# A three-stage fp32 kernel: the last layer's norm moved into factors, its transposes moved into the projection before it, and the pooling products reordered

## The chip, the core and the metric

The kernel runs on one core of one Trainium2 chip. The metric is the device time of one execution in microseconds (us), from the first instruction to the last on that core, with a small part around it. The engines are named as the profile names them: PE is the matrix engine (TensorE), PEld its weight loads, DVE the vector engine, ACT the scalar (activation) engine, POOL GpSimd, and SP the engine that issues nearly all transfers. Everything is fp32. In the trace one fp32 matmul of the program is two rows (two passes over the moving operand); a transpose is one row.

## The reference

The input `x` is 256 tokens by 1024 features. It passes through one block (a gated delta-rule mixer, a mixture of 32 experts, a gated embedding) and then two more layers. Only the ends of the chain matter here, where the change is:

```python
# first mixer: per-token gates are 64 of the input projection's columns
qkv, z, ab = jnp.split(x @ w_in, [GDN_CONV_CH, GDN_CONV_CH + GDN_VAL_WIDTH], axis=-1)
...
def even_layer(x, g_norm, w_in, conv_w, b_if, g_head, w_pool, s_pool, w_out):
    ...
    h = rmsnorm(h, g_head).reshape(bsz, s_len, A_WIDTH).astype(x.dtype)
    y_a = h * jax.nn.silu(z_a)
    pooled = multiscale_pool(u).astype(x.dtype)
    y_b = jnp.einsum('bsgc,gcd->bsgd', pooled, w_pool).reshape(bsz, s_len, B_WIDTH)
    y_b = y_b * s_pool * jax.nn.silu(z_b)
    return x + jnp.concatenate([y_a, y_b], axis=-1) @ w_out

def odd_layer(x, g_norm, w_in, g_kv, w_uk, w_uv, g_q, g_k, w_out, rel_bias):
    xn = rmsnorm(x, g_norm)
    p = xn @ w_in
    q, ckv, qi, ki, wi, z = _split(p, ODD_SPLITS)
    q = rmsnorm(q.reshape(hd), g_q)
    ckv = rmsnorm(ckv, g_kv)
    ...
    return x + (out * jax.nn.silu(z)) @ w_out
```

In the part of the odd layer that is left out, index scores pick 64 keys for each token, and attention runs over those. `rmsnorm` divides each token's row by the root of its mean square. `pooled` has four groups of 256 channels, each with a window of its own; `w_pool` is a 256x256 matrix for each group.

## The kernel before, in words

The program is written out by hand: each engine has its own list of instructions, and `wait_ge` on a semaphore is the only thing that orders them against each other. Nothing is scheduled by a planner; on each engine the order in the source is the order on the chip. Tokens lie in two tiles of 128 (`NT` is 2), features in eight tiles of 128 (`KT` is 8). The accumulators are eight banks of 512 columns, `bank(b)`. Weights come in units of 1 MB (1024x256) into slots; `fill` in `odd_sync`, `even_sync` and elsewhere has SP wait until a slot's last unit is multiplied and then issue the transfer of the next one. SP's list is in order too.

**The start** (`gdn_tensor`, L596 to L606). PE first computes the per-token gates (64 columns): 16 matmuls with tokens as the stationary operand and 64 moving columns (L601). Then come the four halves of head 0's query and key projection (`project_half`, L449, 16 matmuls with 256 moving columns). Then the sums over the gates (L613 on), for which DVE and ACT have meanwhile made the decays.

**The even layer's end** (`even_tensor` from L2264, `even_scalar` from L2356, `even_vector` from L2461). For each of the four groups, PE multiplies by the window matrix (pooling, L2271), ACT copies the bank to SBUF (L2359), and PE multiplies by the group's mixing matrix (L2279); DVE multiplies the result by the silu gate (L2465). After the last group ACT squares the heads (L2368) and makes the root of the mean (L2371, L2373), and DVE scales and gates the heads (L2471). The pooled half `zb` and the head half `za` are transposed by PE (`turn_tensor`, L267) and copied by ACT with a per-feature scale (`turn_scalar`, L281) into `yt`. Only then does the output projection start (`project`, L251): four groups of 256 columns, each with 32 matmuls over both halves of `yt`. DVE adds each group to the residual `x` (L2477).

**The odd layer's head** (`odd_sync` from L2536, `odd_tensor` from L2555, `odd_scalar` from L2755, `odd_vector` from L2874). When the last group is added, SP issues four small transfers and ACT squares all of `x` (L2181) and makes the root. DVE scales `x` by it (L2876), PE transposes the result (L267), ACT copies it with the per-feature weight (L281), and PE multiplies: a small bias product (L2560), the index queries (L2567), the index keys (L2571) and index weights (L2575, 4 moving columns each), and the compressed keys (L2580). The index scores (L2591) follow, then the query projection (L2603), the attention loop with the gate projection in between (L2634), and the output projection (L2695). `keep_gates` (L2808, L2809) brings one unit of the gate projection from its bank to SBUF, once as it is and once through Exp.

## Time and profile before

| What | Value |
|---|---|
| Runs | 1180.51, 1181.7 and 1182.4 us; median 1181.7 us |
| The profiled execution | 1179.04 us, of which 1177.4 us are the span in the trace |
| PE | busy 1076.1 us, 91% of the span |
| DVE, ACT, POOL | busy 33%, 30% and 4% of the span |
| Chain that ended last | PE 76%, SP's queue 10%, DVE 5%, ACT 4%, DMA 3% |
| Mean granted clock of PE | 0.962 of full speed |

The profiled execution took 2.7 us less than the median of the three runs. The chain is read back from the last instruction: at each step to what released it, or to the instruction before it on its engine. It runs through PE nearly everywhere; the question for an edit is where it leaves PE.

### The profile page before, as it was taken

What the parts mean: (1) busy time and instruction counts of PE and PEld (TensorE: products, weight loads), DVE (VectorE), ACT (ScalarE), POOL (GpSimd) and SP (SyncE); (2) the same over time, 40 slices, a digit from 0 to 9 for tenths busy, and PEclk for the clock granted to TensorE, in tenths of its full rate; (3) what the DMA queues carried; (4) which work ended last, traced back from release to release, by engine and by line L of the source; (5) the groups of instructions that cost most, each with busy time, mean ns of one, the idle gap of its engine ahead of it and who ended that gap; (6) DMA issues with size and microseconds to landing.
All of it is one profiled execution on the core that took longest, in us unless ns stands there. A gap on an engine that the chain in (4) does not pass through costs nothing.

```text
span 1177.4 us, 24312 instructions
## 1 busy us (share of the span) xinstructions
PE 1076.1 (91%) x10643; PEld 821.0 (70%) x10643; DVE 391.3 (33%) x937; ACT 354.0 (30%) x988; POOL 43.8 (4%) x47
## 2 busy tenths in 40 slices
PE   7999999999899999887777999999999797999989
PEld 6776777767677884433332788888887686776877
DVE  2555565555552143100000444420001100083760
ACT  2654554644644221110001131031112501033440
POOL 0110000000000000000000000000000000032000
PEclk9999999999999999988888999999999898799989
DMA  6233233233217477999999633434443144431211
GB/s 261 71 138 118 74 119 118 74 118 109 110 45 303 147 275 301 421 421 424 423 422 424 272 105 131 143 112 168 149 144 107 71 149 174 109 143 72 108 36 36
DMA packets 40030, 210.40 MB, mean 179 GB/s; under 512 B 5344, under 2 KB 14432, under 8 KB 15984
## 3 DMA queue, kind: packets, MB, share of 16 engines
q1 hardware_dynamic: 39920, 208.80, 46.7%
q8 instruction: 86, 1.41, 0.5%
q14 instruction: 24, 0.20, 0.1%
HBM read 207.67 MB, written 1.11 MB: 177 GB/s over the span
## 4 chain that ended last, share of the span: by engine, by line
PE 76%; SPq 10%; DVE 5%; ACT 4%; DMA 3%; issue 2%; ACTq 0%; DVEq 0%
SPq L236 10%; PE ps L2299 9%; PE ps L449 9%; PE ps L251 7%; PE ps L452 4%; PE ps L2205 4%; PE ps L2695 3%; PE ps L769 2%; PE ps L2603 2%; PE ps L780 2%; PE ps L2036 2%; DMA arena<-in_wu 2%; PE ps L2634 2%; PE ps L505 2%; PE ps L1541 2%
## 5 line engine op out<-in xcount | busy, mean ns | idle before, releaser
L449 PE MATMUL ps<-xt,slots 128*128 128x256 f32 x512 | 127.1, 395 | 0.0
L2299 PE MATMUL ps<-slots,yt 128*128 128x256 f32 x512 | 110.7, 379 | 0.0
L449 PEld LDWEIGHTS ps<-xt,slots 128*128 128x128 f32 x512 | 94.7, 194 | 19.6 <-issue 7.5
L2299 PEld LDWEIGHTS ps<-slots,yt 128*128 128x128 f32 x512 | 97.2, 190 | 13.2
L251 PE MATMUL ps<-slots,yt 128*128 128x256 f32 x384 | 83.4, 379 | 1.0 <-ACT yt L281 1.0
L251 PEld LDWEIGHTS ps<-slots,yt 128*128 128x128 f32 x384 | 72.8, 190 | 11.0 <-ACT yt L281 1.2
L1541 PE MATMUL ps<-arena 128*32 128x512 f32 x280 | 56.5, 693 | 23.4 <-DMA arena<-in_wu 9.1
L452 PE MATMUL ps<-slots,xt 128*128 128x256 f32 x256 | 64.5, 395 | 0.0
L1092 DVE SCALAR_TENSOR_TENSOR arena<-arena 128x256 f32<-128x256 f32 x128 | 56.2, 485 | 0.3
L452 PEld LDWEIGHTS ps<-slots,xt 128*128 128x128 f32 x256 | 46.5, 192 | 10.6 <-issue 4.3
L1541 PEld LDWEIGHTS ps<-arena 128*32 128x32 f32 x280 | 15.3, 124 | 53.0 <-issue 53.0
L1541 PE MATMUL ps<-slots,arena 128*32 128x512 f32 x160 | 46.2, 734 | 4.4 <-DMA xt<-in_wu 4.4
L2205 PE MATMUL ps<-yt,slots 128*128 128x256 f32 x224 | 49.0, 380 | 0.0
L2205 PEld LDWEIGHTS ps<-yt,slots 128*128 128x128 f32 x224 | 42.3, 190 | 6.1 <-issue 0.4
L3000 POOL TENSOR_TENSOR arena<-arena 128x512 f32<-128x512 f32 (+1 forms) x8 | 17.8, 2260 | 711.2 <-DVE arena L2895 711.2
L2347 ACT ACTIVATE arena<-ps,rms 128x256 f32<-128x256 f32 x32 | 13.4, 471 | 90.2 <-PE ps L2299 90.2
L2459 DVE SCALAR_TENSOR_TENSOR arena<-ps,arena 128x256 f32<-128x256 f32 x8 | 3.2, 477 | 108.5 <-ACT arena L2355 108.5
L1641 ACT ACTIVATE arena<-ps 128x256 f32<-128x256 f32 x8 | 3.1, 386 | 115.1 <-PE ps L1541 115.1
L1314 POOL TENSOR_TENSOR arena<-arena 128x256 f32<-128x256 f32 x32 | 24.3, 761 | 311.7 <-ACT arena L835 193.2
L1862 DVE TENSOR_TENSOR arena<-arena,ps 128x256 f32<-128x256 f32 x8 | 3.4, 422 | 94.0 <-ACT arena L1641 94.0
L2634 PE MATMUL ps<-slots,xt 128*128 128x256 f32 x128 | 31.9, 395 | 1.2 <-ACT arena L2802 1.2
L769 PE MATMUL ps<-slots,yt 128*128 128x256 f32 x128 | 31.0, 389 | 0.0
(397 smaller groups left out, 1788.0 us busy)
## 6 DMA issues: line engine op xcount, KB each, us to landing
slots<-in_wu SPq DMA_DIRECT2D x114, 1024.0 KB, 4.8
arena<-in_wu SPq DMA_DIRECT2D x58, 1024.0 KB, 26.1
yt<-in_wu SPq DMA_DIRECT2D x10, 1024.0 KB, 26.4
xt<-in_wu SPq DMA_DIRECT2D x4, 1024.0 KB, 26.5
arena<-bias_rows SPq DMA_DIRECT2D x1, 2048.0 KB, 14.7
arena<-delta_rows SPq DMA_DIRECT2D x14, 128.0 KB, 7.6
xt<-in_xt SPq DMA_DIRECT2D x2, 512.0 KB, 4.9
x<-in_x SPq DMA_DIRECT2D x1, 1024.0 KB, 8.1
```

The lines of the kernel that those rows point to most:

```text
L236: SP.dma_start(self.slot(slot), self.ins["wu"][unit]).then_inc(*self.arrived[slot].up())
L251: q = M.matmul(self.bank(base + cg, UC, t * UC), lhs[:, h * KT + k, t * P:(t + 1) * P], self.slot(s)[:, k, :], start=(t == 0 and k == 0 an ...
L449: q = M.matmul(bank(n, T), self.slots[:, s, k, n * P:(n + 1) * P], self.xt[:, k, :], start=(k == 0), stop=(k == KT - 1))
L452: q = M.matmul(bank(n, UC), folded(k, n), self.slots[:, s, k, :], start=(k == 0), stop=(k == KT - 1))
L769: q = M.matmul(self.out_bank(t, cg), self.yt[:, k, t * P:(t + 1) * P], self.slots[:, s, k, :], start=((cg % 2 == 0 or (t, cg) == (1, 3)) a ...
L1092: q = V.scalar_tensor_tensor(g.cn[:, s], src, w, g.cn[:, s], ALU.mult, ALU.add)
L1314: G.tensor_tensor(by_cc(g.mt), by_cc(g.ac), g.lvt[:, l].unsqueeze(1).to_broadcast([P, 2, 128]), ALU.mult).then_inc(*g.masked.up())
L1541: q = M.matmul(self.ps[r, 2, :], g.xg[:, half * (KT // 2) + k, r], self.flat(slots[e])[:, k * 512:(k + 1) * 512], start=(half == 0 and k = ...
L2205: q = M.matmul(bank(s, T, T * n), self.slots[:, s, k, n * P:(n + 1) * P], self.xe[:, k, :], start=(k == 0), stop=(k == KT - 1), skip_group ...
L2299: q = M.matmul(self.bank(s, UC, t * UC), self.xe[:, k, t * P:(t + 1) * P], self.slots[:, s, k, :], start=(t == 0 and k == 0), stop=(k == K ...
L2634: q = M.matmul(bank(g.z_banks[u], UC, t * UC), self.xt[:, k, t * P:(t + 1) * P], self.slots[:, u, k, :], start=(t == 0 and k == 0), stop=( ...
L2695: q = M.matmul(bank(g.out_banks[i], UC, t * UC), self.xt[:, k, t * P:(t + 1) * P], self.slots[:, i, k, :], start=(t == 0 and k == 0), stop ...
```

## The change

1. **Start.** The gates are computed with the 64 gate columns as the stationary operand and all 256 tokens moving (8 matmuls), copied by DVE (L1216 of the new file) and transposed back by PE (L607) after a quarter of the first projection.
2. **Pooling ahead of mixing.** The pooling product of the next group stands ahead of the mixing product of each group, in `even_tensor`.
3. **Heads' root later, table earlier.** ACT's activation table with Ln and Exp is loaded once after the sigmoid. ACT copies the transposed `zb` before it makes the heads' root.
4. **Output projection begins with the pooled half.** It is split into half units (8 matmuls each, `out_half`), with an own bank for each column group. Three of them stand ahead of the transposes of `za`. The weights are fetched in the order in which the slots come free now.
5. **Raw x turned.** `turn_columns` transposes each group of `x` as soon as its residual is added, between half units; ACT copies with the norm's per-feature weight, and squares the group.
6. **The norm as factors.** The odd layer's products use `x` without the division by the root. Each consumer gets the factor: index keys by a product with a row of factors (spread by 2 matmuls, L2647 of the new file), index weights by the factor squared, the gates by a per-token scale in `keep_gates`, and the query and compressed-key norms by an epsilon scaled with the token's mean square.
7. The index weights and the small bias table are loaded during the even layer; the mask constants and feature weights stay where the even layer has them.

The diff, cut to its core:

```diff
@@ -596,14 +597,18 @@
         for half in range(2):
             M.wait_ge(*g.xt_in[half](1))
-            for cc in range(2):
-                for k in range(4 * half, 4 * half + 4):
-                    q = M.matmul(bank(2, 64, cc * 64), folded(k, cc), g.wab[:, k, :],
-                                 start=(cc == 0 and k == 0), stop=(k == KT - 1), skip_group_check=True)
+            for k in range(4 * half, 4 * half + 4):
+                q = M.matmul(ps[0:64, 3, 0:T], g.wab[:, k, :], self.xt[:, k, :], start=(k == 0), stop=(k == KT - 1))
+        q.then_inc(*g.gates_f.up())
+        project_half(0, 0, 0)
+        M.wait_ge(*g.gates_fk(1))
+        M.wait_ge(*g.common(3))
+        for cc in range(2):
+            q = M.transpose(bank(2, 64, cc * 64), g.sq[0:64, 0, tile(cc)], ident[0:64, 0:64])
         q.then_inc(*g.gates.up())
-        for j in range(2):
-            for part in range(2):
-                project_half(0, j, part)
+        project_half(0, 0, 1)
+        project_half(0, 1, 0)
+        project_half(0, 1, 1)
...
@@ -2168,22 +2181,14 @@
+        SP.wait_ge(*g.scores(1))
+        SP.dma_start(self.wki[:, :, :], I["w_ki"]).then_inc(*self.odd_in.up())
+        SP.dma_start(self.rb[:, :], I["rel_bias_2"]).then_inc(*self.odd_in.up())
         for s in (4, 5):
             self.fill(s, U_CKV + s - 4)
-        for i in range(2):
-            for s in range(4):
+        for i, order in enumerate(((1, 3, 0, 2), (1, 0, 3, 2))):
+            for s in order:
                 self.fill(s, U_EOUT + 4 + 4 * i + s)
...
@@ -2279,14 +2290,62 @@
+        pool(0)
+        pool(1)
+        mix(0)
+        pool(2)
+        mix(1)
+        pool(3)
+        mix(2)
+        mix(3)
...
+        def out_half(cg, h, t):
+
+            s = (2 * cg + h) % 4
+            if t == 0:
+                M.wait_ge(*self.arrived[s](self.multiplied[s].n + 1))
+            for k in range(KT):
+                q = M.matmul(bank(cg, UC, t * UC), self.yt[:, h * KT + k, t * P:(t + 1) * P], self.slots[:, s, k, :],
+                             start=(h == 1 and t == 0 and k == 0), stop=(h == 0 and k == KT - 1), skip_group_check=True)
...
         M.wait_ge(*g.zb_made(4))
         M.wait_ge(*g.hn_made(2))
-        self.turn_tensor(g.pj[:, 2], KT, [6, 7], g.zb_turned, g.zb_kept)
+        self.turn_tensor(g.pj[:, 2], KT, [4, 5, 6, 7], g.zb_turned, g.zb_kept)
+        M.wait_ge(*g.zb_kept(4))
+        out_half(0, 1, 0)
+        out_half(0, 1, 1)
+        out_half(1, 1, 0)
         M.wait_ge(*g.za_made(1))
-        self.turn_tensor(g.pj[:, 1], KT, [4, 5], g.za_turned, g.za_kept)
+        self.turn_tensor(g.pj[:, 1], KT, [4, 5, 6, 7], g.za_turned, g.za_kept)
+        out_half(1, 1, 1)
         M.wait_ge(*g.za_kept(4))
-        g.out_done = self.project(self.yt, 8, 2, self.even_added)
+        for cg in range(2):
+            out_half(cg, 0, 0)
+            out_half(cg, 0, 1)
+        self.turn_columns(0)
+        for cg in range(2, 4):
+            out_half(cg, 1, 0)
+            out_half(cg, 1, 1)
+            self.turn_columns(cg - 1)
+            out_half(cg, 0, 0)
+            out_half(cg, 0, 1)
+
+    def turn_columns(self, c):
+
+        M = self.nc.tensor
+        M.wait_ge(*self.even_added(c + 1))
+        for j in range(2):
+            for t in range(NT):
+                q = M.transpose(self.bank(4 + c, P, j * T + t * P), self.x[:, t, (2 * c + j) * P:(2 * c + j + 1) * P],
+                                self.c["ident"])
+        q.then_inc(*self.x_turned.up())
...
@@ -2353,6 +2412,7 @@
         A.activation(g.pj[:, 3], g.pj[:, 3], ACT.Sigmoid).then_inc(*g.o_sig.up())
+        A.preload_act_table_set("natural_log_exp_and_others")
...
@@ -2535,11 +2605,6 @@
-        SP.wait_ge(*self.even_added(4))
-        SP.dma_start(g.late_at, I["c_late"]).then_inc(*g.loaded.up())
-        SP.dma_start(g.wki[:, :, :], I["w_ki"]).then_inc(*g.loaded.up())
-        SP.dma_start(g.feat[:, :], I["feat"]).then_inc(*g.loaded.up())
-        SP.dma_start(g.rb[:, :], I["rel_bias_2"]).then_inc(*g.loaded.up())
...
@@ -2554,19 +2619,21 @@
-        M.wait_ge(*g.xn_made(1))
-        self.turn_tensor(g.xn, KT, [0, 1], g.turned, g.xt_kept)
-        M.wait_ge(*g.loaded(4))
...
+        for cg in range(4):
+            M.wait_ge(*self.x_kept(cg + 1))
+            for n in range(2):
+                for k in (2 * cg, 2 * cg + 1):
+                    q = M.matmul(bank(5, T, n * T), self.slots[:, 5, k, n * P:(n + 1) * P], self.xt[:, k, :],
+                                 start=(n == 0 and k == 0), stop=(k == KT - 1), skip_group_check=True)
+            if cg == 0:
+                self.turn_columns(3)
...
+        M.wait_ge(*g.diag_made(1))
+        for t in range(NT):
+            q = M.matmul(bank(0, P, t * P), c["ones"], g.diag[:, t], start=True, stop=True, skip_group_check=True)
+        q.then_inc(*g.r_spread.up())
...
@@ -2805,8 +2880,11 @@
-            A.activation(g.pq[:, 1, :, cols], self.two(g.z_banks[u]), ACT.Copy)
-            A.activation(g.pq[:, 0, :, cols], self.two(g.z_banks[u]), ACT.Exp, scale=-1.0).then_inc(*g.z_kept.up())
+            for t in range(NT):
+                src = bank(g.z_banks[u], UC, t * UC)
+                A.activation(g.pq[:, 1, t, cols], src, ACT.Copy, scale=r[:, t:t + 1])
+                q = A.activation(g.pq[:, 0, t, cols], src, ACT.Exp, scale=g.neg[:, t:t + 1])
+            q.then_inc(*g.z_kept.up())
...
@@ -2871,11 +2951,23 @@
         V.wait_ge(*g.st_exp(1))
         for t in range(NT):
-            q = V.tensor_scalar(g.xn[:, t], self.x[:, t], g.st[:, t:t + 1], None, ALU.mult)
-        q.then_inc(*g.xn_made.up())
-        V.wait_ge(*g.loaded(4))
+            q = V.tensor_scalar(g.diag[:, t], c["ident"], r[:, t:t + 1], None, ALU.mult)
+        q.then_inc(*g.diag_made.up())
+        V.tensor_scalar(g.neg[:, :], r, -1.0, None, ALU.mult)
+        V.scalar_tensor_tensor(g.rr[:, :], r, IH ** -0.5, r, ALU.mult, ALU.mult).then_inc(*g.rr_made.up())
+        V.wait_ge(*g.index_kept(1))
+        V.wait_ge(*g.r_spread(1))
+        V.tensor_tensor(g.kit[:, :], g.kit[:, :], bank(0, T), ALU.mult).then_inc(*g.kit_made.up())
```

How the edits move instructions is seen in three pieces of the engines' lists. PE at the even layer's end, before: L2271 pools, L2279 mixes, L267 transposes both halves of `yt`, L251 is the output projection.

```order
L2279 MATMUL ps<-slots,arena 128x256 x4
L2271 MATMUL ps<-slots,arena 128x256 x4
L2279 MATMUL ps<-slots,arena 128x256 x4
L267 MATMUL ps<-cst,arena 128x128 x32
L251 MATMUL ps<-slots,yt 128x256 x128
```

The same place in the changed kernel: L2290 mixes, L267 transposes `zb` and then `za`, L2311 is `out_half`, L2346 transposes raw `x`, and L2630 is the index query product of the odd layer.

```order
L2290 MATMUL ps<-slots,arena 128x256 x8
L267 MATMUL ps<-cst,arena 128x128 x16
L2311 MATMUL ps<-slots,yt 128x256 x24
L267 MATMUL ps<-cst,arena 128x128 x16
L2311 MATMUL ps<-slots,yt 128x256 x40
L2346 MATMUL ps<-cst,x 128x128 x4
L2311 MATMUL ps<-slots,yt 128x256 x16
L2346 MATMUL ps<-cst,x 128x128 x4
L2311 MATMUL ps<-slots,yt 128x256 x32
L2346 MATMUL ps<-cst,x 128x128 x4
L2311 MATMUL ps<-slots,yt 128x256 x16
L2630 MATMUL ps<-xt,slots 128x256 x4
```

The 128 matmuls of the projection are still 128, but 24 of them stand ahead of the second 16 transposes, and 12 of the 16 transposes for the odd layer stand among them.

PE at the odd layer's head, before (L267 transposes the normed `x`):

```order
L267 MATMUL ps<-cst,arena 128x128 x16
L2560 MATMUL ps<-arena 16x512
L2567 MATMUL ps<-xt,slots 128x256 x16
L2571 MATMUL ps<-xt,arena 128x256 x8
L2575 MATMUL ps<-arena,xt 128x4 x16
L2580 MATMUL ps<-slots,xt 128x256 x16
```

And in the changed kernel, from the index query product on:

```order
L2630 MATMUL ps<-xt,slots 128x256 x4
L2346 MATMUL ps<-cst,x 128x128 x4
L2630 MATMUL ps<-xt,slots 128x256 x12
L2635 MATMUL ps<-arena 16x512
L2638 MATMUL ps<-xt,arena 128x256 x8
L2642 MATMUL ps<-arena,xt 128x4 x16
L2647 MATMUL ps<-arena,cst 128x128 x2
L2651 MATMUL ps<-slots,xt 128x256 x16
```

Four transposes are left here, after the first quarter of the index queries; the small bias product stands behind them, and two matmuls that spread the factors are new.

ACT from the pooled copies on, before (L281 copies transposed blocks, L2181 squares `x`):

```order
L2359 ACTIVATE arena<-ps 128x512 x4
L2368 ACTIVATE arena<-arena 128x256 x8
L2371 ACT_TABLE_LOAD
L2371 ACTIVATE arena<-arena,cst 128x8
L2373 ACT_TABLE_LOAD
L2373 ACTIVATE arena<-arena 128x8
L281 ACTIVATE yt<-ps,arena 128x256 x16
L2757 ACT_TABLE_LOAD
L2181 ACTIVATE arena<-x 128x1024 x2
L2184 ACTIVATE arena<-arena,cst 128x2
L2186 ACTIVATE arena<-arena 128x2
L281 ACTIVATE xt<-ps,arena 128x256 x8
```

And in the changed kernel (L2439 copies a column group of transposed `x`, L2443 squares it; both come four times, of which one is shown):

```order
L2415 ACT_TABLE_LOAD
L2419 ACTIVATE arena<-ps 128x512 x4
L2428 ACTIVATE arena<-arena 128x256 x8
L281 ACTIVATE yt<-ps,arena 128x256 x8
L2432 ACTIVATE arena<-arena,cst 128x8
L2434 ACTIVATE arena<-arena 128x8
L281 ACTIVATE yt<-ps,arena 128x256 x8
L2439 ACTIVATE xt<-ps,arena 128x256 x2
L2443 ACTIVATE arena,rms<-x 128x256 x2
```

One table load ahead of the copies takes the place of three behind the squares, and the copies of `zb` stand ahead of the root.

## Rows read from the trace of the kernel before

**Rows 1.** The page's first line.

```profile
span 1177.4 us, 24312 instructions
```

**Rows 2.** Timeline, first 22 us: start, duration, engine, line, operation, count.

```profile
5.06 0.43 SPq L373 DMA_DIRECT2D arena<-in_gdn_norm_w  x1
...
5.79 7.06 PE L601 MATMUL ps<-arena,xt 128*128 128x64 f32 x32 [5.79 <-DMA xt<-in_xt]
...
12.64 8.34 PE L449 MATMUL ps<-xt,slots 128*128 128x256 f32 x32
...
15.02 0.19 DVE L1228 COPY arena<-arena 64x64 f32<-64x64 f32 x1
...
20.91 0.28 PE L613 MATMUL ps<-arena 64*64 64x16 f32 x2
```

**Rows 3.** Weight loads at the start, by line: min/median/max ns, first and last start.

```profile
L601 PEld LDWEIGHTS ps<-arena,xt x32: 285/333/333, 5.8 to 12.3; 128*128 128x128 f32 x32
L449 PEld LDWEIGHTS ps<-xt,slots x32: 190/190/337, 12.5 to 20.4; 128*128 128x128 f32 x32
```

**Rows 4.** Transfers, first 40 us and 895 to 1035 us: KB, median us to landing.

```profile
arena<-in_gdn_norm_w SPq DMA_DIRECT2D x1, 0.5 KB, 6.8
...
slots<-in_wu SPq DMA_DIRECT2D x13, 1024.0 KB, 4.8
```

**Rows 5.** Chain that ended last, even layer's end: start, duration, what.

```profile
904.26 1.74 PE ps L2271 x8
...
906.68 1.99 PE ps L2279 x8
...
919.75 1.70 ACT arena L2368 x8
...
923.27 1.28 ACT L2371
...
926.42 3.27 DVE arena L2471 x8
...
934.56 55.53 PE ps L251 x256
```

**Rows 6.** Timeline of the same stretch: DVE gates, PE transposes, ACT copies.

```profile
921.93 0.69 DVE L2465 TENSOR_TENSOR arena<-arena,ps 128x512 f32<-128x512 f32 x1 [3.72 <-PE ps L2279]
...
922.67 1.09 PE L267 MATMUL ps<-cst,arena 128*128 128x128 f32 x8 [0.78 <-DVE arena L2465]
...
926.30 1.55 ACT L281 ACTIVATE yt<-ps,arena 128x256 f32<-128x256 f32 x4
```

**Rows 7.** Chain that ended last, odd layer's head.

```profile
992.32 5.52 DMA arena<-in_rel_bias
...
1000.73 1.81 PE ps L2560 x2
1002.54 10.00 PE ps L2567 x32
1012.54 3.45 PE ps L2571 x16
1016.00 4.12 PE ps L2575 x32
1020.12 9.70 PE ps L2580 x32
```

**Rows 8.** Stretches: us, PE, PEld, DVE, ACT, POOL busy, granted clock, DMA share, GB/s.

```profile
994.70:1008.40 13.70, 11.61 (x32) 8.00 (x33) 0.33 (x1) 3.84 (x9) 0.00 (x0) 0.50 0.34 110
1018.60:1025.40 6.80, 6.80 (x21) 5.72 (x21) 0.00 (x0) 0.94 (x3) 0.00 (x0) 0.50 0.01 3
926.40:933.30 6.90, 5.46 (x23) 4.51 (x24) 3.25 (x8) 5.18 (x13) 0.00 (x0) 0.51 0.00 0
```

**Rows 9.** Chain that ended last, last gate unit in the attention loop.

```profile
1131.88 0.60 ACT arena L2808
...
1132.99 0.44 DVE arena L2931
```

114 lines of the change are left out of this document (72 added, 42 removed).

## The prediction

> **What bounds the kernel now.** I read the page's chain first. It stays on PE for 76% of the span of 1177.4 us [rows 1], so an edit pays only where the chain leaves PE. Then I followed the chain in order of time through the three places that the diff touches.
>
> At the even layer's end it alternates. A pooling product (1.74 us) is followed by ACT's copy of the bank, and the mixing product starts 0.68 us after the pooling product ends; four such rounds take the time from 904.26 to about 919.2 [rows 5]. Then the chain goes over ACT (squares from 919.75, two table loads of 1.28 us between 923.27 and 926.4), over DVE (3.27 us) and over the transposes of the head half, until the output projection starts at 934.56 [rows 5]. It is 55.53 us of PE without a gap, to 990.09. At the odd layer's head PE is off the chain again: the last of four small transfers is issued at 992.32 and lands 5.52 us later, and the first index query matmul stands at 1002.54 [rows 7]. In this stretch PE's granted clock falls: 0.50 from 994.7 to 1008.4, 0.50 again from 1018.6 to 1025.4, and 0.51 from 926.4 to 933.3 [rows 8]. So 1.2 GHz instead of 2.4, and a matmul pass takes twice its time.
>
> Prices of PE's work. At full clock a pass with 256 moving columns is 55.53/256 = 0.217 us [rows 5]. A program matmul is two passes, 0.434 us; eight of them (an `out_half`) are 3.47 us. At half clock a pass is twice that, 0.434. A transpose is 1.09/8 = 0.136 us [rows 6], so four are 0.54 and sixteen 2.2 us.
>
> **The start.** Before, 32 passes with 64 moving columns take 7.06 us, and the four projection halves 8.34 us instead of 32 x 0.217 = 6.9 [rows 2]. Weight loads take 333 ns in the first passes and 190 ns later [rows 3], so PE begins at the pace of half clock, and 8.34 - 6.9 = 1.4 us lost means that the pace doubled 2.8 us after 12.64 less half a pass, near 15. After, 16 passes with 256 moving columns cost 16 x 0.434 = 6.9 us: from 5.79 to 12.7, as long as before. The first half projection is 8 passes, five at the slow pace and the rest at the fast one, to 15.6. The constants that the transposes wait for are in by 5.06 + 6.8 = 11.9 [rows 2, 4], so this wait costs nothing; if the gates were ready at 9.2 it would cost 0 to 1 us. Two transposes, 0.3 us; then 24 passes, 5.2 us: the sums start at 21.1 instead of 20.91 [rows 2]. The gates' own chain on DVE and ACT, which ended at 15.2 for gates made at 12.8, ends near 18.3, ahead of 21.1. Term: **+0.2 us**. When the pace doubles need not stay the same, since PE's work ahead of it is another: if it came at 11.5 instead of 15, 3.5 us of slow work would run in half the time, and the term would be 0.2 - 1.75 = -1.5 us. That is the other bound.
>
> The Trainium skill ("TensorE: Matmul & The Clock Gate", section "What's actually happening") says that the engine's default is the throttled state and that activity releases it. The loads of 333 ns agree [rows 3], although the granted clock is listed as full there.
>
> **The even layer's end.** PE: pool 0, pool 1, mix 0, pool 2, mix 1, pool 3, mix 2, mix 3. Each ACT copy (0.68 us with its hand-over) now lies under another product of 1.74 us, so eight products run on: 8 x 1.74 = 13.9 us, from 904.26 to 918.2. The last gate by DVE (0.69 us, [rows 6]) makes `zb` ready at 918.95. ACT copies the last bank by 915.4 and squares from there for 3.52 us (919.75 to 923.27 before, [rows 5]), to 918.9: just as late as `zb`. The early table load needs 1.28 us beside PE's first pooling and costs nothing; if it were not covered it would cost that. PE transposes `zb`, the first group of four by 919.5, all by 921.2. ACT copies 16 blocks' worth in 8 activations, 2 x 1.55 = 3.1 us [rows 6] plus hand-overs, to 922.9. This is what ends last: the projection starts at **922.9 instead of 934.56, -11.7 us**. Behind the copies, Ln and Exp (0.5 us, no table load between) and DVE's 3.27 us [rows 5] give `za` at 926.7. PE gets there after three half units, 922.9 + 10.4 = 933.3, so 6.6 us are spare.
>
> What moves into the projection: 16 transposes of `za` (2.2 us) and 12 of raw `x` (3 x 0.54 = 1.6). The copies of `za` (3.3 us) lie under half a unit that takes 3.47: cover is just enough, up to 0.3 us could show. ACT's copies and squares of `x` lie under 13.9 us of PE a group. The projection ends at 922.9 + 55.5 + 2.2 + 1.6 = **982.2, against 990.09: -7.9 us**.
>
> The weights: slots 1 and 3 are freed at 929.8 and 938.9, slots 0 and 2 at 945.8 and 952.8, and their next units are wanted at 953.3 and 967.7, 960.7 and 975. A unit lands in 4.8 us [rows 4]; the tightest has 14.9. Nothing is added. SP's new wait on the scores stands behind 28 weight units, long after the scores; the small transfers behind it delay the next unit by an issue each, under the same margin.
>
> **The odd layer's head.** The root, DVE's scaling, twelve transposes, all copies and the four small transfers leave the path. PE goes on: index queries 16 x 0.434 = 6.9, four transposes 0.54 (the last residual add, 0.7 us, is hidden by the first quarter, 1.7), so 989.7; bias product at full clock 1.81/2 = 0.9, to 990.6; index keys 3.45; index weights 4.12 [rows 7]; spreading the factors 0.5, to 998.7. The factors themselves (squares, sums, Ln, Exp on ACT and DVE) end near 988.5. Compressed keys: 9.70 as before [rows 7], if the clock falls again, else 6.9.
>
> I take 9.70; the other bound is 6.9. The fall at 1018.6 came 2.6 us into the 32 passes with 4 moving columns, which ran back to back [rows 7, 8], and those passes are unchanged. So 1008.4 instead of 1029.8: this part gives 39.7 - 26.2 = **-13.5 us**. Of that, 4.0 is clock (the index queries from 10.00 to 6.9, the bias product from 1.8 to 0.9); the rest is idle time and transposes.
>
> The same page of the Trainium skill has the clock fall for an idle PE. The row speaks against it, since PE was not idle before 1018.6. By the page there would be no fall and the term would be 2.8 us larger.
>
> DVE's scaling of the index keys (0.4 us, after ACT's copies by 999.7) is hidden by the compressed keys. From the scores on all waits keep their distances: selection on DVE, bias tiles and weights are all started by events that move along.
>
> **The tail.** Copies of the gates are four activations of 256 columns instead of two of 512: 1.55 [rows 6] instead of about 1.1 (1131.88 to 1132.99, [rows 9]). The last one is on the chain, for DVE and ACT alike. **+0.5 us**; if all four counted, +1.9. The second Ln for the queries and for the compressed keys (0.3 each) lie beside 7 us and more of PE.
>
> **Sum.** +0.2 - 7.9 - 13.5 + 0.5 = -20.7 us. On the profiled execution that is 1179.04 - 20.7 = 1158.3; that one took 2.7 us less than the median of 1181.7, so for the median of the runs **1161 us**.
>
> **The rivals.**
>
> A. *The clock is kinder.* No fall in the compressed keys, or an earlier release at the start. For it: the narrow passes now end 0.5 us of 128-column work earlier than the next wide ones, and when the clock changes is not tied to the program. Against: the row of before. 1161 - 2.8 = 1158, with both 1156.5. Chance 0.22.
>
> B. *The clock falls once more.* PE now waits about 0.8 us for `zb` and 1.7 for its copies, with 2.2 us of transposes between. A fall like that of 926.4 to 933.3 costs half of 6.9, 3.4 us. For it: that fall came in just such a place. Against: before that fall PE stood from 923.8 [rows 6], longer than either wait here. 1164.5. Chance 0.14.
>
> C. *Part is given back in the attention loop*, by the longer gate copies on every round (+1.4 more) and by selection, which on DVE ends before the keys' transposes with little to spare. Some 3 to 7 us back, 1164 to 1168. Chance 0.08.
>
> D. *The edit does not do what it says*: `za` becomes late or a weight unit does, and the projection, once begun, stops again for as long as it started earlier. That is 6.6 us spare for `za` and 14.9 for weights; PE would stand for 11.7 us more. Only the odd head's 13.5 and the tail are left: about 1173. Chance 0.03.
>
> E. *Slower than before*: PE starts the projection at half clock after the broken-up stretch and keeps it. Each us of time at half clock loses half a us, so 20.7 us are eaten after 41.4 us at half clock; over the whole projection, 55.5 us more of time, less 20.7: 1216. The longest fall in these rows is 13.7 us [rows 8]. Chance 0.02.
>
> The forecast has 0.51. About 0.2% (2.4 us) is what a measurement of this kernel can tell from no change. All cases but E and a part of the unforeseen lie far below 1179.3: faster 0.96, same 0.01, slower 0.03. The range for 8 in 10 takes in A, the forecast with 2 us either way for the term of the start and for the run-to-run spread, and B and the near part of C: **1155.5 to 1167**.
>
> **What would show it.** In the changed file, L2279 and L2290 (pooling, mixing) without idle time on PE, and zb's copies ending near 922.9 on the old scale; three times 16 passes of `out_half` ahead of the transposes of `za`, and no wait at them; the projection ending near 982; no idle time of PE between it and the index scores but at the hand-over to the scores; the compressed keys at about 9.7 us with a granted clock of 0.5 in part; the first sums at 21 us. The prediction is wrong if PE waits for `za` or a slot in the projection, if the clock falls at its start, or if the attention loop is more than 2 us longer than before.

## The result, and the profile after

The changed kernel takes 1150.01 us (median of four runs, 1146.79 to 1153.66) against 1181.14 us for the kernel before in the same rounds (1180.51 to 1182.4). The ratio is 0.9743, with a 95% interval of 0.9713 to 0.9773: 31 us less. The forecast was 1161, range 1155.5 to 1167. The sign is right, the time lies below the stated range, and a third of the gain is missing from the forecast.

The profiled execution took 1146.79 us. It is the fastest of the four; the forecast for it was 1158.3. The page's span, PE line and chain:

```profile
span 1145.5 us, 24320 instructions
...
PE 1058.1 (92%) x10633; PEld 807.0 (70%) x10633; DVE 391.2 (34%) x945; ACT 354.1 (31%) x1009; POOL 44.4 (4%) x47
...
PE 77%; SPq 10%; DVE 5%; ACT 3%; DMA 3%; issue 2%; DVEq 0%; ACTq 0%
```

The span is 31.9 us shorter [rows 1]. To divide it I took the same events in both traces. All times are from the first instruction.

| Stretch | Before | After | Difference | Forecast |
|---|---|---|---|---|
| Start to first gate sums | 20.91 | 18.58 | -2.3 | +0.2 |
| From there to the first pool product | 883.35 | 879.94 | -3.4 | 0 |
| First pool product to the end of the even projection | 85.83 | 76.95 | -8.9 | -7.9 |
| From there to the end of the compressed keys | 39.7 | 24.57 | -15.2 | -13.5 |
| From there to the end of the span | 147.6 | 145.5 | -2.1 | +0.5 |

The timeline of PE in the first 20 us of the changed kernel answers to [rows 2], and its row of weight loads (PEld) to [rows 3]:

```profile
6.03 5.05 PE L601 MATMUL ps<-xt,arena 128*64 128x256 f32 x16 [6.03 <-DMA xt<-in_xt]
8.62 2.00 PEld L601 LDWEIGHTS ps<-xt,arena 128*64 128x64 f32 x9 [0.20 <-issue]
11.01 1.99 PE L450 MATMUL ps<-xt,slots 128*128 128x256 f32 x8
12.93 0.34 PE L607 MATMUL ps<-cst,arena 64*128 64x64 f32 x2
13.20 5.45 PE L450 MATMUL ps<-xt,slots 128*128 128x256 f32 x24
18.58 0.28 PE L618 MATMUL ps<-arena 64*64 64x16 f32 x2
```

The 16 passes of L601 take 4.98 us to the next line, not 16 x 0.434 = 6.9. The eight behind them are already near the full pace (1.92 us to the next line, against 8 x 0.217 = 1.74). If s passes were slow, 4.98 = s x 0.434 + (16 - s) x 0.217, so s is 7, and the pace doubled about 3 us after 6.03, near 9.1. The weight loads agree: from 8.62 on nine of them follow each other in 2.00 us. In the kernel before the pace doubled near 15.

The chain that ended last, from the first pool product (start, duration, what) answers to [rows 5, 7], and its last two rows to [rows 9]:

```profile
898.52 3.45 PE ps L2279 x16
901.98 1.73 PE ps L2290 x8
...
908.88 3.47 PE ps L2290 x16
...
912.37 0.70 DVE arena L2534
...
913.11 0.67 PE ps L267 x4
...
913.81 3.03 ACT yt L281 x8
...
916.88 10.63 PE ps L2311 x48
927.51 1.75 PE ps L267 x16
929.26 17.27 PE ps L2311 x80
...
975.47 1.73 PE ps L2630 x8
977.20 0.44 PE ps L2346 x4
977.64 5.18 PE ps L2630 x24
982.82 0.96 PE ps L2635 x2
983.77 3.65 PE ps L2638 x16
987.42 3.47 PE ps L2642 x32
990.89 0.55 PE ps L2647 x4
991.44 8.60 PE ps L2651 x32
...
1101.17 0.47 ACT arena L2885
...
1102.77 0.44 DVE arena L3023
```

Eight pool and mix products run without a gap for 13.8 us. Then come the last gate on DVE (0.70), one group of transposes (0.67) and ACT's eight copies (3.03). The projection starts 18.36 us after the first pool product, where it was 30.3 [rows 5]. From there PE is on the chain without a gap for 83.2 us, until the compressed keys end at 1000.04. PE gets to the transposes of `za` (L267) at 927.51 and does not wait.

Four stretches with their PE clock (columns as in [rows 8]): two in the first mixer of the kernel before, then one in the mixer of the changed kernel and one in its compressed keys. Before:

```profile
257.40:260.90 3.50, 3.50 (x20) 2.08 (x13) 2.34 (x8) 0.00 (x0) 0.00 (x0) 0.51 0.02 7
318.90:325.70 6.80, 5.20 (x79) 4.19 (x80) 1.48 (x3) 3.24 (x13) 1.06 (x2) 0.50 0.01 4
```

After:

```profile
316.40:319.80 3.40, 3.40 (x12) 2.44 (x8) 0.00 (x0) 1.88 (x9) 0.22 (x1) 0.54 0.01 2
992.30:995.70 3.40, 3.40 (x10) 2.70 (x9) 0.26 (x1) 0.00 (x0) 0.00 (x0) 0.55 1.01 330
```

The mixer has 3.4 us at half clock (1.2 GHz) instead of 10.2. No edit touches the program there. Half of the 6.8 us would be 3.4, the second line of the table, but the traces divide it otherwise. From the first sums to the first pass of the mixer's output projection (L769 before, L774 in the changed kernel) it takes 333.6 us before and 329.9 after, 3.7 less. One instruction of DVE that comes again and again (L1141 before, L1146 in the changed kernel) shows where. It starts 2.2 us earlier in the changed kernel at 54 and at 111 us, 3.3 earlier at 135 and at 240, 5.5 at 266 and 6.1 at 327 (times of before). So 1.1 of the 3.7 us came at full clock, 2.2 around the first fall of before and 0.6 around the second.

The fall in the compressed keys is still there, but lasts 3.4 us and not 6.8. In the tail it is 6.8 us (from 1104.6 and 1111.4) instead of 10.2 (from 1117.6 and 1141.5).

So two questions stood open. Why does the start give 2.3 us, and what has the mixer's clock to do with it? And is the even layer's end, with the head behind it, what the forecast said it was?

### The profile page after: what moved, and what is told of

Same layout as the page of the kernel before. It is cut to its first block, busy times and chain, and to the rows that moved or that the text cites. A ratio compares the mean times of both kernels' runs of the same rounds, so it can differ in the third digit from the quotient of the medians.

```text
span 1145.5 us, 24320 instructions
## 1 busy us (share of the span) xinstructions
PE 1058.1 (92%) x10633; PEld 807.0 (70%) x10633; DVE 391.2 (34%) x945; ACT 354.1 (31%) x1009; POOL 44.4 (4%) x47
## 3 DMA queue, kind: packets, MB, share of 16 engines
HBM read 207.12 MB, written 1.11 MB: 182 GB/s over the span
## 4 chain that ended last, share of the span: by engine, by line
PE 77%; SPq 10%; DVE 5%; ACT 3%; DMA 3%; issue 2%; DVEq 0%; ACTq 0%
SPq L236 10%; PE ps L2358 10%; PE ps L450 9%; PE ps L2311 5%; PE ps L453 5%; PE ps L2210 4%; PE ps L774 2%; PE ps L2766 2%; PE ps L2674 2%; PE ps L785 2%; PE ps L2043 2%; PE ps L251 2%; DMA arena<-in_wu 2%; PE ps L2705 2%; PE ps L506 2%
## 5 line engine op out<-in xcount | busy, mean ns | idle before, releaser
L2358 PE MATMUL ps<-slots,yt 128*128 128x256 f32 x512 | 110.7, 379 | 0.0
L2358 PEld LDWEIGHTS ps<-slots,yt 128*128 128x128 f32 x512 | 97.2, 190 | 13.2
L1548 PE MATMUL ps<-arena 128*32 128x512 f32 x280 | 54.8, 687 | 26.2 <-DMA arena<-in_wu 10.3
L2311 PE MATMUL ps<-slots,yt 128*128 128x256 f32 x256 | 56.2, 379 | 1.8 <-ACT yt L281 1.8
L2311 PEld LDWEIGHTS ps<-slots,yt 128*128 128x128 f32 x256 | 48.2, 190 | 8.4 <-ACT yt L281 2.0
L1548 PEld LDWEIGHTS ps<-arena 128*32 128x32 f32 x280 | 14.8, 124 | 55.5 <-issue 55.5
L1588 PE MATMUL ps<-arena 128*32 128x512 f32 x152 | 24.7, 678 | 8.2 <-issue 5.1
```

The costliest lines, as they stand in the source:

```text
L1548: q = M.matmul(self.ps[r, 2, :], g.xg[:, half * (KT // 2) + k, r], self.flat(slots[e])[:, k * 512:(k + 1) * 512], start=(half == 0 and k = ...
L1588: q = M.matmul(self.ps[r, b, :], g.ht[:, f, r], self.flat(slots[e])[:, f * D + b * 512:f * D + (b + 1) * 512], start=(f == 0), stop=(f == ...
L2311: q = M.matmul(bank(cg, UC, t * UC), self.yt[:, h * KT + k, t * P:(t + 1) * P], self.slots[:, s, k, :], start=(h == 1 and t == 0 and k == ...
L2358: q = M.matmul(self.bank(s, UC, t * UC), self.xe[:, k, t * P:(t + 1) * P], self.slots[:, s, k, :], start=(t == 0 and k == 0), stop=(k == K ...
```

## The experiments

Each kernel with a ratio is compared with the kernel before in the same rounds (17 runs of before each time: median 1180.88 for `start_only`, `old_start`, `even_only` and `again`, 1178.66 for `start_delayed`, `narrow_spread` and `both_more`). The others have one run beside one of before (1178.07; `start_wide` stood beside the rounds with 1178.66).

### The start edit alone, and everything but it

`start_only` is the kernel before with change 1 alone; the diff is the first part of the one ahead. `old_start` is the changed kernel without it.

> The kernel before with only the edit at the start (gates by feature, transposed back). In the trace of the changed kernel the first gate sums stand at 18.58 us instead of 20.91, but the mixture stage begins 6 us earlier, not 2.3: the rest fell in the first mixer, where the kernel before had PE at half clock for 10.2 us and the changed one for 3.4. Theory 1 (two things): the edit itself gives 2.3 us, because PE's pace doubles earlier, and the other 3.4 are the clock's own scatter: median 1178 to 1180 us, first sums near 18.6 us, and half-clock stretches in the first mixer that vary from run to run. Theory 2 (one thing): the earlier start changes the spacing in the mixer so that falls are avoided each time: median 1175 to 1176 us. Theory 3, my forecast: +0.2 us, 1181 to 1182 us.

> The changed kernel with the start as before. Theory 1: first sums near 20.9 us, median 2 to 3 us above the changed kernel in the same rounds. Theory 2: 5 to 6 us above it. Theory 3: no difference. In all three the even layer's end and the odd layer's head take as long as in the changed kernel: 18.4 us from the first pooling product to the projection, 58.6 us of projection, 24.6 us to the index scores.

`start_only`: 1174.85 us, ratio 0.9954 [0.9934, 0.9975]. The sums start at 18.82, and the mixer has 3.4 us at half clock (317.2). `old_start`: 1154.71 us, ratio 0.9777 [0.9745, 0.9809]. The sums start at 20.72, and the mixer has 10.2 us at half clock (257.6 and 319.0), at the places of before.

So both effects belong to the start edit. Alone it is worth 6.0 us at the median, where the forecast had +0.2. Within the changed kernel it is worth 3.0 (`old_start` less `again`, below). The two rows of the table, 2.3 and 3.4, sum to 5.7 and lie between. In the trace of `start_only` the sums come 2.1 us earlier than in before and the mixer takes 330.2 us instead of 333.6, and the whole span is 5.4 us shorter.

### The even layer's end alone

`even_only` is the kernel before with the pool order, the early table, the split projection and the order of its weights; `x` is not turned early, and the norm is no factor.

```diff
+        A.preload_act_table_set("natural_log_exp_and_others")
...
+        M.wait_ge(*g.zb_kept(4))
+        out_half(0, 1, 0)
+        out_half(0, 1, 1)
+        out_half(1, 1, 0)
         M.wait_ge(*g.za_made(1))
-        self.turn_tensor(g.pj[:, 1], KT, [4, 5], g.za_turned, g.za_kept)
+        self.turn_tensor(g.pj[:, 1], KT, [4, 5, 6, 7], g.za_turned, g.za_kept)
+        out_half(1, 1, 1)
```

> The kernel before with only the even layer's end changed: pooling ahead of mixing, the table load early, the projection in half units from the pooled half on, weights in the new order. The residual add, the odd layer's norm, transposes and small transfers are as before. Theory 1: first pooling product to projection 18.4 us instead of 30.3, projection 55.5 plus 1.75 for the transposes of the head half, so 10.1 us less than before: median 1171 us. The odd head stays at 39.7 us with its half clock. Rival: most of what the projection gains is lost again in it (head half late, slots late): 1173 to 1178 us with idle time of PE inside the projection.

Measured: 1169.53 us, ratio 0.9902 [0.9867, 0.9937], 11.4 us less. Its chain:

```profile
907.38 3.45 PE ps L2273 x16
...
925.75 10.63 PE ps L2305 x48
936.38 1.75 PE ps L267 x16
```

Pool to projection is 18.37 us, just as in the changed kernel. The projection ends at 983.04, 75.7 us after the first pool product (85.83 before): 10.2 us by the trace. The odd head stays 39.7 us, as before. In the same rounds `old_start`, which adds the turned `x` and the factors, is 14.8 us faster than `even_only`. The parts add up within the noise: their medians sum to -6.0 - 11.4 - 14.8 = -32.2, and `again` lies 29.1 below before.

### The changed kernel once more

`again` is the changed kernel, with no edit.

> The changed kernel once more, unchanged. Four runs gave 1146.8 to 1153.7 us with mean granted clocks from 0.979 down to 0.967, while four of the kernel before lie within 2 us. Theory 1: times follow the clock; a run with more half-clock stretches is longer by half of their length, so 0.01 of mean clock is worth some 5 to 11 us, and the profile of this kernel has other stretches than the first one at the same code. Rival: the spread is of another source, for instance the transfers of the expert weights, and times do not follow the clock.

1151.75 us, ratio 0.9762 [0.9729, 0.9794]; mixer 3.4 us at half clock. The result stands. From the first pool product to the end of the compressed keys its trace takes 101.52 us, just as in the first trace of this kernel. The tail does not repeat: 148.2 us, where the first trace has 145.5 and before 147.6. Its half clock is 10.2 us, not 6.8 (columns as in [rows 8]):

```profile
1088.40:1091.80 3.40, 3.40 (x13) 2.26 (x10) 2.79 (x7) 2.08 (x8) 0.00 (x0) 0.50 0.33 135
1112.30:1119.10 6.80, 6.80 (x28) 6.17 (x27) 0.69 (x1) 0.60 (x1) 0.00 (x0) 0.50 0.01 2
```

So the shorter tail of the first trace is the scatter of one execution and not an effect of the edit.

### The pool order alone

`pool_only` is the kernel before with the order pool 0, pool 1, mix 0, pool 2, mix 1, pool 3, mix 2, mix 3, and nothing else.

> The kernel before with the eight pooling and mixing products in the new order and nothing else. By my working the last mixing product ends 13.9 us behind the first pooling product instead of 17.6, and ACT's squares end 4.4 us earlier than before; the rest of the chain (two table loads, DVE, transposes, copies, also at half clock) stays, so the projection starts 25.9 to 26.6 us behind the first pooling product instead of 30.3. Rival: the pooled half's transposes were what held the chain, not the squares; then 3.7 us.

One run, 1177.16 us, against 1178.07 of before. Its chain:

```profile
906.74 3.45 PE ps L2273 x16
...
917.63 1.70 ACT arena L2382 x8
...
924.31 3.27 DVE arena L2485 x8
...
927.62 1.13 PE ps L267 x4
...
932.53 2.64 PE ps L251 x11
```

Pool to projection is 25.8 us, against 30.3 [rows 5] and 18.36. The order alone gives 4.5 us. The other 7.4 come mostly from what stood behind the squares: ACT's root, its two table loads, DVE's scaling. In the changed kernel these lie under the first three half units. About 0.9 of the 7.4 is clock: `pool_only` has 0.50 from 924.6 to 931.4, and there two groups of transposes on the chain take 1.13 us each instead of 0.67.

### The table loads back at their place

`late_tables` is the changed kernel with the table of Ln and Exp no longer loaded early.

```diff
         A.activation(g.pj[:, 3], g.pj[:, 3], ACT.Sigmoid).then_inc(*g.o_sig.up())
-        A.preload_act_table_set("natural_log_exp_and_others")
...
         A.activation(g.mm[:, 5], g.mm[:, 5], ACT.Exp, scale=-0.5).then_inc(*g.h_exp.up())
+        A.preload_act_table_set("natural_log_exp_and_others")
         self.turn_scalar(self.yt[:, 0:8], KT, [4, 5, 6, 7], g.za_turned, g.za_kept, g.fcol(F_HEAD))
```

> The changed kernel without the table load behind the sigmoid: as before, one load stands ahead of Ln, one ahead of Exp and one behind it. My working had 6.6 us to spare for the head half and called the early load free. So: the head half ready 2.6 us later (near 923.2 on the scale on which the projection starts at 916.9), still ahead of the transposes at 927.4, projection start and end unchanged, and no difference of time beyond the scatter of the clock. Rival: loads delay ACT's copies of the pooled half or of the head half; then PE waits at the head half's transposes or behind them for up to 2.6 us.

One run, 1148.05 us. Timeline:

```profile
917.90 1.28 ACT L2431 ACT_TABLE_LOAD   x1
...
917.93 10.63 PE L2311 MATMUL ps<-slots,yt 128*128 128x256 f32 x48 [1.81 <-ACT yt L281]
...
919.51 1.28 ACT L2433 ACT_TABLE_LOAD   x1
```

The first load begins when the projection does. `za` is ready at 924.3, and PE comes to its transposes at 928.56: 4.3 us spare instead of 7.0, and no wait. The early table is worth nothing in this order: with the `zb` copies ahead of the root, the loads lie under the projection.

### Where PE's pace doubles: wide gates

`start_wide` is the kernel before with each gate product moving four copies of the gate columns; the extra columns are not read.

```diff
-                    q = M.matmul(bank(2, 64, cc * 64), folded(k, cc), g.wab[:, k, :],
+                    q = M.matmul(bank(2, 256, cc * 256), folded(k, cc), g.wab[:, k, :].unsqueeze(1).to_broadcast([P, 4, 64]),
```

> The kernel before, whose 16 gate products at the start move four copies of the 64 gate columns (256 moving columns instead of 64, three copies are not used); the passes stay 32. My forecast's view, that PE keeps the slow pace until about 15 us whatever it does: the gates end at about 5.8 + 21 slow passes of 0.434 + 11 fast ones of 0.217 = 17.4 us, the sums stand at about 24.4. The view from the changed kernel, in which the pace doubled at 9 to 10 us with this kind of pass: 8 to 10 slow passes, the gates end near 14.7 and the sums stand near 21.6 us.

One run, 1180.06 us. Timeline:

```profile
5.76 8.96 PE L601 MATMUL ps<-arena,xt 128*128 128x256 f32 x32 [5.76 <-DMA xt<-in_xt]
14.56 7.07 PE L449 MATMUL ps<-xt,slots 128*128 128x256 f32 x32
21.56 0.28 PE L613 MATMUL ps<-arena 64*64 64x16 f32 x2
```

64 passes of 256 columns take 15.8 us. All fast they would take 13.9; the 1.9 us more are nine slow passes, so the pace doubled near 9.6, 3.8 us after the first wide pass. A pace that doubles at 15 whatever PE does would have put the sums at 24.4. What PE does at the start decides when its pace doubles. By the same working it came 3.0 us after the first pass in the changed kernel, 3.9 in `start_only` and 4.2 in `again`, and with 64-column passes 9.2 us after it in before and 11.1 in `pool_only`. Over all traces it is 3.0 to 4.3 us in the ten that begin with 256 columns and 9 to 11 us in the four that begin with 64.

The earlier doubling gave this kernel nothing, since its wide passes cost more than it saved: the sums start at 21.56, and its mixer takes 334.0 us and has 10.2 us at half clock.

### Is it the time of the sums that decides the mixer's clock?

`start_delayed` is `start_only` with five products of 256 columns, whose results nobody reads, ahead of the gate sums. `delay_1` and `delay_3` have one and three.

```diff
         project_half(0, 1, 1)
+        for k in range(5):
+            M.matmul(bank(7, T), self.xt[:, k, 0:P], self.xt[:, k, :], start=True, stop=True)
         M.wait_ge(*g.gate_g(1))
```

> The kernel of start_only, with five more products of 256 columns into an unused bank ahead of the gate sums, which nobody reads: work of 2.2 us that puts the sums back to about 21.0 us, where the kernel before has them, while PE's pace still doubles near 10 us. Three traces with the old start have half clock in the first mixer at 257 and 319 us (10.2 us in all), three with the new start only at 317 (3.4 us). Theory 2 (the distance between the pace's doubling and the work decides): the falls at 257 and 319 may come back or not; what matters is the distance of the sums from the doubling, 11 us here, 8.6 with the new start and 5.8 with the old. Theory 2a, only the work's time decides: 10.2 us of half clock again and a median 5 to 6 us above start_only, that is 1180 to 1181. Theory 2b, the earlier doubling decides: 3.4 us of half clock and 2.2 us above start_only, 1177. Theory 1 (scatter): either, without a pattern.

> start_only with one unread product (0.43 us) ahead of the gate sums instead of none; start_delayed had five (2.2 us) and its half clock in the first mixer was 10.2 us, at 40 and 316 us, against 3.4 us in all traces without delay. If the mixer's half clock hangs on how its short pauses of PE lie in time, it changes with the delay and not in proportion: 3.4 or 10.2 here, and 0.4 us later sums. If it is decided by the earlier doubling of the pace alone, it is 3.4.

> The same with three unread products (1.3 us). As for delay_1: either 3.4 or 10.2 us of half clock in the mixer; the two together show from which delay on the falls come. A smooth growth with the delay (5 and 8 us, say) would speak for a cause that has nothing to do with the timing of pauses.

| Kernel | Sums start | From there to the mixer's output projection | Mixer at half clock | Time, us |
|---|---|---|---|---|
| start_only | 18.82 | 330.2 | 3.4 (317.2) | 1174.85 (12 runs) |
| delay_1 | 18.98 | 330.7 | 3.4 (316.5) | 1174.35 (one run) |
| delay_3 | 20.68 | 331.6 | 6.8 (317.4) | 1177.85 (one run) |
| start_delayed | 20.68 | 331.5 | 10.2 (40.0, 316.5) | 1181.46 (12 runs) |
| start_wide | 21.56 | 334.0 | 10.2 (40.2, 320.1) | 1180.06 (one run) |

Two rows of `start_delayed` with the PE clock (columns as above):

```profile
40.00:43.40 3.40, 3.40 (x8) 2.38 (x8) 1.95 (x4) 3.03 (x5) 0.83 (x1) 0.51 0.03 7
316.50:323.30 6.80, 5.09 (x79) 4.16 (x80) 1.59 (x3) 3.34 (x13) 1.16 (x2) 0.51 0.01 4
```

`start_delayed` has a ratio of 1.0014 [0.9991, 1.0038]: five unread products, 2.3 us of work, took back the whole gain of 6 us. Its trace shows only about half of that. The span is 3.1 us longer than that of `start_only` (1175.1 against 1172.0): the sums come 1.9 us later and the mixer takes 1.3 us more. The profiled execution (1176.71) is among the fastest of the twelve.

The half clock returned, but 6.8 us more of it made the mixer 1.3 us longer and not 3.4. Its length at half clock is therefore no measure of what it costs. The places are no mark of the start either: `pool_only`, with the start of before, has its falls at 40.6 and 320.5, and not at 257 and 319.

`delay_1` and `start_delayed` make a clean pair, with one trace each: PE begins at 5.66 and 5.62, and the pace doubles near 9.4 in both. Only the unread products differ, one against five, and the half clock is 3.4 against 10.2. `delay_3`, whose sums start at the same 20.68 as those of `start_delayed`, has 6.8, which neither of my alternatives foresaw. In its trace PE began 0.7 us later (6.35), so it isn't quite the same program start.

The traces of all kernels sort well by the start. Those with the old one (before, `old_start`, `even_only`, `pool_only`) have 10.2 us of half clock in the mixer, four of four, and take 333.3 to 334.0 us for it. Those with the new one and little or no delay (after, `again`, `start_only`, `delay_1`, `late_tables` and the next two kernels) take 329.9 to 330.7; six of the seven have 3.4 us of half clock and `late_tables` has 6.8. That the start edit shortens the mixer and lowers its half clock is shown. By what path is not: where PE's work lies in time matters, and the time of the sums alone does not fix it.

### The narrow passes spread out

`narrow_spread` is the changed kernel with the 16 index weight products (4 moving columns each) put between the index key products, two behind each, instead of all behind them.

```diff
         for k in range(KT):
             M.matmul(bank(6, T), g.wki[:, k, 0:P], self.xt[:, k, :], start=(k == 0), stop=(k == KT - 1),
                      skip_group_check=True)
-        for t in range(NT):
-            for k in range(KT):
+            for t in range(NT):
                 q = M.matmul(bank(6, IH, T + t * IH), self.xt[:, k, t * P:(t + 1) * P], g.wki[:, k, P:P + IH],
-                             start=(k == 0), stop=(k == KT - 1), skip_group_check=True)
+                             start=False, stop=(k == KT - 1), skip_group_check=True)
```

> The changed kernel with the 32 passes of 4 columns (index weights) no longer in one piece, but four after each two passes of the index keys. In all traces so far the clock fell in or just after that piece (at 1018.6, 992.3, 998.3, 1013.5, 1011.6 and 993.2 us), though PE did not stand still. If the piece is the cause: no fall between the projection's end and the scores, compressed keys 6.9 us instead of 8.6, index queries to scores about 1.7 us shorter, median 1 to 2 us below the changed kernel. If the cause lies elsewhere (in the load on PE as a whole, or in chance): the fall stays, and the stretch with it. By the clock page of the Trainium skill, a fall comes from idleness; then nothing here would change it.

1149.49 us, ratio 0.9755 [0.9724, 0.9785]. The stretch from the projection's end to the index scores, columns as in [rows 8], and the compressed keys in the chain:

```profile
976.00:999.20 23.20, 23.15 (x124) 19.53 (x122) 2.20 (x10) 3.91 (x14) 0.00 (x0) 1.00 0.61 171
```

```profile
992.30:995.70 3.40, 3.40 (x17) 3.01 (x16) 0.42 (x1) 0.60 (x4) 0.00 (x0) 1.00 1.04 303
```

```profile
992.24 6.91 PE ps L2650 x32
```

The clock stays at 1.00, and the compressed keys take 6.91 us instead of 8.60. The head is 22.88 us long against 24.57: 1.7 us less, for the same products in another order. The transfers are not what brings the clock down: in the same 3.4 us the changed kernel has 330 GB/s at half clock and this one 303 at full clock, and the fall of before came beside 3 GB/s [rows 8]. It is not chance either. In all twelve traces with the narrow passes in one piece the clock falls during the piece or up to 1.2 us behind it; in the two that spread them, this one and the next, it does not fall there. The back-to-back narrow passes are what it hangs on here.

The 1.7 us are read from the traces. The time of the whole kernel is too coarse for them: 0.9755 here and 0.9762 for `again` lie well within each other's intervals.

### Transposes of `zb` group by group, too

`both_more` is `narrow_spread` with each group of `zb` turned by itself when its gate is ready, two of the four ahead of the last mixing product, and ACT's copies of them between its two rounds of squares.

```diff
         mix(2)
+        M.wait_ge(*g.hn_made(2))
+        turn_pooled(0)
+        turn_pooled(1)
         mix(3)
+        turn_pooled(2)
+        turn_pooled(3)
```

> narrow_spread, and the transposes of the pooled half taken group by group: two of them stand ahead of the last mixing product, and ACT copies all four between its squares of the first and of the second token tile. In the changed kernel PE waits 0.8 us for the last gate and 1.8 for ACT's copies. Expected: the projection starts 15.3 to 15.6 us behind the last window product's group copies as before, that is 16.9 us after the first pooling product instead of 18.4; the head half is still ready ahead of its turn. Together with the narrow passes 3 us below the changed kernel, 1147 to 1149 us. Rival: the head half comes late because its squares are split, and PE stops for it; then the 1.5 us are given back.

1146.24 us (1145.35 to 1147.6), ratio 0.9727 [0.9699, 0.9756]. Chain:

```profile
898.64 3.45 PE ps L2279 x16
...
910.73 0.87 PE ps L2298 x8
911.60 1.74 PE ps L2290 x8
...
913.37 0.70 DVE arena L2555
...
914.11 0.67 PE ps L2298 x4
...
915.70 10.63 PE ps L2324 x48
```

Pool to projection is 17.06 us instead of 18.36. ACT's copies are off the chain but for the last, and 0.87 us of transposes came on. It is the fastest kernel of the study, 3.3 us below `narrow_spread` in the same rounds, of which its trace explains 1.3; the rest is open.

## Why the prediction was right in sign and in its two large terms, and too small

The profiled execution was forecast at 1158.3 and took 1146.79: 11.5 us off. By the table of the first section, 2.5 of it are in the start, 3.4 behind it, 1.0 in the even end, 1.7 in the odd head, 2.6 in the tail, and 0.3 in what lies around the span.

**The start: the step that failed.** It read that the pace doubled near 15 us in the trace of before, and priced all 16 wide passes at the slow pace, "from 5.79 to 12.7". Measured: the gates done at 11.0, the pace doubled at 9.1, the sums at 18.58 instead of 21.1. The text saw that the time of doubling need not stay, and set 11.5 as the other bound, -1.5 us. It came earlier still: 2.3 us. `start_wide` shows that the kind of pass is what moved it: the doubling came 3.8 us after the first pass with 256 columns, and 9.2 with 64. The reading of the weight loads (333 ns at the slow pace) was right, and the constants at 11.9 cost no wait.

**The sum's silence about the mixer: the second step that failed.** The sum had terms for edited places only. The 883 us from the first gate sums to the first pooling product stood at nothing, without a reason. Measured: 3.7 us came in the first mixer, up to 300 us behind the edit (1.1 at full clock, the rest around the two falls of before), and 0.3 were lost again behind it, 3.4 in all. `old_start` and `start_only` tie it to the start; the path stays open. I had an extra fall and a kinder clock as rivals, but both at edited places. Rival A (1156.5 with both its parts) points the right way, and one of its parts came, the earlier release at the start; its size is still 6.5 us short of the measured median.

**The even end: right, 1.0 us too small.** Pool to projection: forecast 30.3 to 18.6, measured 18.36. `zb`'s copies end it, as said. `za` was ready at 920.5 and had 7.0 us to spare against 6.6. The projection with its transposes takes 58.59 us against 59.3: four transposes in a run of matmuls cost 0.44 us, not 0.54. PE does wait 0.78 us for the last gate and 1.80 for the copies, and no fall of the clock follows (rival B did not come). `pool_only`, `even_only` and `late_tables` confirm the parts: 4.5 from the order, 7.4 mostly from moving root and scaling under the projection, and 0 from the early table.

**The odd head: right, 1.7 us too small.** Every row of the chain is where the forecast has it. The index queries with their four transposes, bias product and index keys are within 0.3 us. Two sizes were off: the index weights, 3.47 instead of 4.12 (they ran at full clock), and the compressed keys, 8.60 instead of 9.70. The fall came as in [rows 8], but near 992, just behind the narrow passes, and for 3.4 us. The Trainium skill ("TensorE: Matmul & The Clock Gate", section "What's actually happening") ties the fall to an idle engine. This case's trace does not agree: PE was busy for 3.40 of 3.40 us in the fall and without a gap ahead of it, and `narrow_spread` takes the fall away by order alone, for 1.7 us. The falls in the mixer of before agree better with it: PE was busy for 1.30 of the 3.40 us ahead of 257.4, and for 1.45 of the 3.40 us ahead of 318.9.

**The tail: the term right, the rest scatter.** The last four gate copies take 1.60 us from 1101.17 to the start of DVE's product (1102.77), against 1.11 [rows 9]: +0.5, as said. No larger cost showed in the attention loop (rival C). The tail is still 2.1 us shorter in this trace, but in `again`, the same kernel, it is 0.6 us longer than before, as the forecast has it. So the 2.6 us belong to this one execution. The two traces differ by 3.4 us at half clock, which would be worth 1.7 by half of its length; 1.0 of the 2.7 us between them has no place that I can name.

**Rivals D and E** did not come: no wait at the weights or for `za`, and the projection runs at full clock.

## What to carry to other kernels

A product chain that alternates with copies on another engine is worth staggering by one, and a projection over two halves can begin with the half that is ready: two terms that the trace of before sized within 1 us in 8 and 1.7 us in 13.5. Terms that lie in the clock are another matter. A sum over the edited places leaves out what the rest of the trace does. Here places without an edit gave 3.7 us in the mixer and between -2.1 and +0.6 in the tail, and a small delay at the start took the gain back. So count the half clock of the whole trace first, and let the range say what it could give or take. Take a second trace of the same kernel before reading a difference in an unedited place. Where many matmuls with very few moving columns run back to back, try putting them between wide ones; here that cost nothing and gave 1.7 us in the trace.

## What the runs showed of the hardware that I had not expected

- The first PE work of the kernel runs at half pace. The pace doubled 9 to 11 us after the first pass where passes with 64 moving columns came first (four traces), and 3.0 to 4.3 us after it where passes with 256 did (ten). The granted clock is listed as 1.00 meanwhile.
- 32 passes with 4 moving columns, back to back, came with a fall to 1.2 GHz while PE was busy, during them or up to 1.2 us behind them (at 1018.6 before, near 992 after; twelve of twelve traces). Spread among wide ones, none (two of two).
- An edit in the first 20 us made the mixer 3.7 us shorter, most of it some 240 us and more behind the edit, and took its half clock from 10.2 to 3.4 us. Five unread products in the same place brought the half clock back, elsewhere, but only 1.3 us of the length. The path stays open.
- Runs of one kernel differ by up to 11.6 us (17 runs of before, 1173.37 to 1184.94), and their mean granted clock goes with it: 7 to 10 us for 0.01 of the clock in two sets of 17 runs. One profiled execution can lie some 5 us from the median. Where the clock is the same in both, differences within it are much finer: 101.52, 101.52 and 101.53 us from the first pool product to the end of the compressed keys in the changed kernel, `again` and `late_tables`.
